# A two-block transformer kernel on one core: memory's keys and values moved into the first attention's stream of products, slabs in another order, the first slab split in quarters, and five waits moved to other engines

## The reference, cut to what matters

```python
h = rms_norm(x, g_norm[l]);  z = h @ w_in[l]
q, k, v, fl, gf, u, gs, qm, gm, gl = split_cols(z)
y_fox = forgetting_attention(q, k, v, log_f) * silu(gf)          # 12 heads of 64
y_s5  = gelu(s5_ssm(u, ...))                                      # complex diagonal state, 48 groups
y_s5  = y_s5 * sigmoid(y_s5 @ w_glu[l] + b_glu[l]) * silu(gs)
kv = rms_norm(mem, g_mem_norm[l]) @ w_mem_kv[l];  mk, mv = split(kv)   # mem is 256 x 1024
y_mem = memory_attention(qm, mk, mv) * silu(gm)                   # 4 heads of 128
gates = sigmoid(gl + b_merge[l])
merged = gates[0]*(y_fox @ w_proj_fox) + gates[1]*(y_s5 @ w_proj_s5) + gates[2]*(y_mem @ w_proj_mem)
x = x + merged @ w_out[l]
```

## Time and profile before

| | us |
|---|---|
| median of three runs | 2324.04 |
| lowest, highest | 2322.27, 2328.61 |
| the profiled execution | 2326.38 |
| its span | 2324.6 |
| busy: PE, DVE, ACT, POOL | 2254.0, 1250.6, 626.4, 1702.5 |

### The profile page before, as it was taken

How to read it: one execution, slowest core, us unless ns; L and a number is a source line. 1 busy time by engine, 2 the same in 40 slices (tenths; PEclk the granted TensorE clock), 3 DMA queues, 4 the chain that set the end, 5 groups by cost and what they waited for, 6 DMA issues and landing times.

```text
span 2324.6 us, 31091 instructions
## 1 busy us (share of the span) xinstructions
PE 2254.0 (97%) x11693; PEld 1827.6 (79%) x11693; DVE 1250.6 (54%) x1804; ACT 626.4 (27%) x1272; POOL 1702.5 (73%) x2692
## 2 busy tenths in 40 slices
PE   7998988999999999999999999999999999999999
PEld 5887766777888888777868888878877777888887
DVE  5976345554443675545668576647645365723121
ACT  3233344332222211444223333201135321300000
POOL 6898161198789899534789888989963378899884
PEclk9999999999999999999999999999999999999999
DMA  6455851423555332211345655523321133432321
GB/s 201 120 135 129 266 173 37 136 82 121 158 166 176 124 112 91 69 46 28 124 144 164 197 173 190 182 90 127 106 90 33 28 113 101 143 111 95 105 91 55
DMA packets 268656, 280.87 MB, mean 121 GB/s; under 512 B 29964, under 2 KB 240592, under 8 KB 268508
## 3 DMA queue, kind: packets, MB, share of 16 engines
q1 hardware_dynamic: 245148, 243.76, 33.8%
q10 hardware_dynamic: 23360, 35.13, 4.7%
HBM read 257.87 MB, written 17.85 MB: 119 GB/s over the span
## 4 chain that ended last, share of the span: by engine, by line
PE 88%; POOL 3%; DVE 3%; DMA 2%; ACT 2%; issue 1%; ACTq 1%; SPq 1%; DVEq 0%; POOLq 0%
PE ps L478 48%; PE ps L641 15%; PE ps L2469 4%; PE ps L2470 4%; PE ps L2471 4%; PE ps L949 2%; PE ps L992 2%; POOL ring_low L249 2%; PE ps L968 2%; PE ps L1121 1%; PE ps L1138 1%; PE ps L1145 1%; POOL ring_high L245 1%; DMA ring<-in_w_in_dram 1%; PE ps L2579 1%
## 5 line engine op out<-in xcount | busy, mean ns | idle before, releaser
L249 POOL TENSOR_TENSOR ring_low<-ring,ring_high 128x256 fp32r<-128x256 f32 x1320 | 1039.7, 818 | 28.5
L245 POOL TENSOR_SCALAR ring_high<-ring 128x256 fp32r<-128x256 f32 x1320 | 623.8, 498 | 517.0 <-PE ps L641 192.2
L478 PE MATMUL ps<-hT_high,ring_high 128*128 128x512 f32 x704 | 279.5, 397 | 5.6 <-POOL ring_low L249 4.1
L478 PE MATMUL ps<-hT_low,ring_high 128*128 128x512 f32 x704 | 275.9, 392 | 0.0
L478 PE MATMUL ps<-hT_high,ring_low 128*128 128x512 f32 x704 | 275.0, 391 | 0.0
L641 PE MATMUL ps<-hT_high,ring_high 128*128 128x512 f32 x568 | 236.2, 416 | 14.7 <-POOL ring_low L249 11.2
L641 PE MATMUL ps<-hT_high,ring_low 128*128 128x512 f32 x568 | 227.3, 400 | 0.0
L641 PE MATMUL ps<-hT_low,ring_high 128*128 128x512 f32 x568 | 226.9, 400 | 0.0
L390 DVE TENSOR_REDUCE ada_acc<-ring 128x256 f32<-128x2048 f32 x48 | 188.1, 3918 | 45.9 <-ACT ring L377 45.8
L478 PE MATMUL ps<-hidden_high,ring_high 128*128 128x512 f32 x512 | 201.0, 393 | 0.0
L478 PE MATMUL ps<-hidden_low,ring_high 128*128 128x512 f32 x512 | 199.6, 390 | 0.0
(11 more groups left out here) (399 smaller groups left out, 4000.9 us busy)
## 6 DMA issues: line engine op xcount, KB each, us to landing
ring<-in_w_in_dram SPq DMA_DIRECT2D x75, 1024.0 KB, 5.3
ring<-in_w_ff_dram SPq DMA_DIRECT2D x64, 1024.0 KB, 5.4
ring<-in_w_ada_dram SPq DMA_DIRECT2D x48, 1024.0 KB, 5.4
ring<-in_w_out_dram SPq DMA_DIRECT2D x12, 1024.0 KB, 5.5
scratch_x<-xT ACTq DMA_DIRECT2D x3, 2048.0 KB, 7.9
ring<-in_w_mem_kv_dram SPq DMA_DIRECT2D x4, 1024.0 KB, 6.2
ring<-in_w_branch_a_dram SPq DMA_DIRECT2D x16, 256.0 KB, 4.1
xT<-scratch_x ACTq DMA_DIRECT2D x2, 2048.0 KB, 9.7
```

The lines of the kernel that those rows point to most:

```text
L245: ins = nc.gpsimd.tensor_scalar(x(hi), x(raw), 1.0, 1.0, ALU.mult, ALU.mult)
L249: ins = nc.gpsimd.tensor_tensor(x(lo), x(raw), x(hi).bitcast(F32), ALU.subtract)
L478: return nc.tensor.matmul(out[0:rows, bank, cols[0]:cols[1]], lhsT, rhs, start=start, stop=stop)
```

## The change

1. **First slab.** POOL splits slab 0 in quarters of two k-tiles, both halves of the columns in turn, and TensorE starts the first two tiles on a quarter instead of on both halves. In `load_stage` the copies of x's turned tiles 2 and 3 go from DVE to ACT, and ACT's others are interleaved with the rounding.
2. **Layout DMAs.** For parts 1 to 4, ACT no longer issues the eight DMAs of the table; SP does, at the front of its turn. The table is copied to SBUF earlier. POOL splits one piece of four of the second half of f's slab.
3. **Slabs.** The four ada slabs after glu_z2, the two mk slabs and the first mv slab are moved behind the last merge slab and out slabs 0, 2 and 3. glu_z0 is issued before SP's turn for the last part, and not behind the reload of y.
4. **Memory in the stream.** The eight tiles of keys and values become the last 64 products of the attention's stream, taken by ACT. The gate of y_fox moves into the attention too, one tile in four steps. `paces` is denser.
5. **Split of y_mem.** ACT rounds, DVE subtracts; POOL no longer does.

```diff
@@ split_weights
+    def first_slab():
+        K.slab_here(pool, 0)
+        for q in range(KD // 2):
+            last = q == KD // 2 - 1
+            for c in range(2):
+                raw = K.slot(0)[:, 2 * q:2 * q + 2, c * P:(c + 1) * P]
+                hi, lo = (x[:, 2 * q:2 * q + 2, :] for x in K.half(0, c))
+                nc.gpsimd.tensor_scalar(hi, raw, 1.0, 1.0, ALU.mult, ALU.mult).then_inc(...)
+                nc.gpsimd.tensor_tensor(lo, raw, hi.bitcast(F32), ALU.subtract).then_inc(...)
...
+        if i == K.first["f"] and c == 1:
+            pieces = pieces[:1]
@@ plan_slabs
     for i in range(3):
         add(f"glu_z{i}", T["w_glu"][0], (0, 768), 0, 768, False, part=i)
-        if i != 1:
+        if i == 0:
             ada(0)
...
         add("mk", T["w_mem_kv"][0], dm, 0, 512, False, part=i)
-        ada(0)
     for i in range(2):
         add("mv", T["w_mem_kv"][0], dm, 512, 512, False, part=i)
-        if i < 1:
-            ada(0)
...
-            if (mp, b) != (3, 2):
-                ada(0)
+            ada(0)
     for i in range(4):
         add("out", T["w_out"][0], dm, 0, D, part=i)
-        if i == 1:
-            ada(0)
+        ada(0)
@@ tiles_stage (VectorE)
+                    early = ada.get(n, []) if n == 0 and arriving is not None else []
+                    for s in early:
+                        ada_add(K, e, s)
@@ s5_stages
     def next_turn(sp, n):
         sp.wait_ge(y_made.sem, n + 1)
-        if n == PARTS - 2:
-            lay_last(sp)
+        if n + 1 < PARTS:
+            lay_next(sp, n + 1)
...
-        K.sync_turns.setdefault(min(slab_at(out_at[n]) + 3, K.first["glu_z0"]), []).append(lambda sp, n=n: next_turn(sp, n))
-    K.sync_turns.setdefault(K.first["glu_z0"], []).append(lambda sp: load_y(sp, PARTS - 1))
+        K.sync_turns.setdefault(min(slab_at(out_at[n]) + 3, K.first["glu_z0"] + (n == PARTS - 1)), []).append(
+            lambda sp, n=n: next_turn(sp, n))
+    K.sync_turns.setdefault(K.first["glu_z0"] + 1, []).append(lambda sp: load_y(sp, PARTS - 1))
...
-                if n < PARTS - 1:
+                if n == 0:
                     lay_toeplitz(n)
                 else:
-                    stream.take(e, out_at[n] - 48)
+                    stream.take(e, pad_at[n] if n < PARTS - 1 else out_at[n] - 48)
@@ fox_stages
+        if n == 10:
+            e.wait_ge(scored.sem, scored0 + 8)
+        if n < 14:
+            return nc.scalar.activation(K.mk[:, n - 10, :], x[:, 0:MEM], ACT.Copy)
+        i, t = divmod(n - 14, 2)
+        return nc.scalar.activation(K.mv[:, t, i * SLAB_W:(i + 1) * SLAB_W], x[:, 0:SLAB_W], ACT.Copy)
...
+    tiles += column_tiles(K, K.first["mk"], 4, KD, K.memT, n=MEM)
...
-            pe.wait_ge(taken.sem, taken.total - len(late))
...
-            for s in late:
-                ada_sum(K, pe, s, 4)
...
+    def gate_of(e, i):
+        m, at = divmod(i - 6, 4)
+        if m >= 0 and at == 0:
+            e.wait_ge(tanh.sem, m + 1)
+            e.wait_ge(out_copied.sem, out0 + 4 * m + 4)
+            gate(K, e, K.y_fox[:, m, :], K.xT[:, m, :], th[:, m % 2, :]).then_inc(gated.sem, 1)
+    paces = [84, 96]
+    for i in range(1, 26):
+        paces.append(min(paces[-1] + (14, 10, 10, 10)[i % 4] if paces[-1] < 235 else paces[-1] + (8, 5, 5, 6)[i % 4], 304))
     attention_stage(K, steps, ..., K.first["gf"], stream,
-                    [84] + [96 + 11 * i // 2 for i in range(24)] + [230, 240, 240])
+                    paces + [304], beside=(tanh_of, gate_of))
@@ mem_stages
-    tiles_stage(K, tiles, 1, dve=dve, also=also, ada_bank=6, late=last, ada_lag=5)
...
-    def split_mem(pool):
-        pool.wait_ge(gated.sem, gated.total)
-        for k in range(12, 16):
-            split_tile(pool, k)
...
+            for k in range(12, 16):
+                e.wait_ge(gated.sem, gated.total - 15 + k)
+                nc.scalar.activation(highs[k], rows_of[k], ACT.Copy).then_inc(mem_rounded.sem, 1)
...
+                v.tensor_tensor(lows[k], rows_of[k], highs[k].bitcast(F32), ALU.subtract).then_inc(mem_split.sem, 1)
@@ load_stage
+    by_scalar = (2, 3, 6, 7, 4, 5)
...
-            evict(2)
-            evict(3)
-            e.wait_ge(by_dve.sem, 4)
+            e.wait_ge(by_dve.sem, 2)
```

More of the change, by code:

```diff
@@ L613, in __init__ @@
         self.seen = set()
-        self.size = len(tiles[0])
+        self.ends = list(itertools.accumulate(len(t) for t in tiles))
         for n, t in enumerate(tiles):
@@ L619, in __init__, with whole @@
         self.taken.total += len(tiles)
+    def whole(self, upto):
+        return sum(1 for end in self.ends if end <= upto)
     def feed(self, pe, upto):
@@ L625, in feed @@
         while self.fed < upto:
-            n, j = divmod(self.fed, self.size)
+            n = self.whole(self.fed)
+            j = self.fed - (self.ends[n - 1] if n else 0)
             if self.arriving is not None and n < 2:
@@ L630, in feed @@
                 if x == 0:
+                    if k % 2 == 0 and k < KD - 2:
+                        pe.wait_ge(K.sig("first_slab_split").sem, k + 2)
+                    if k == KD - 2:
+                        for c in range(2):
+                            K.weight_here(pe, (0, c))
+                            self.seen.add((0, c))
                     pe.wait_ge(self.arriving[0].sem, self.arriving[1] + k + 1)
@@ L636, in feed @@
                     pe.wait_ge(self.taken.sem, self.t0 + before[-1] + 1)
-            if key not in self.seen:
+            if key not in self.seen and (self.arriving is None or n >= 2):
                 self.seen.add(key)
@@ L646, in take @@
     def take(self, e, upto):
-        while (self.took + 1) * self.size <= upto:
+        while self.took < self.whole(upto):
             n = self.took
@@ L861, in norm_stage, with attention_stage @@
     return low, l0, before, 1
-def attention_stage(K, steps, probs, turned, first_slab, stream=None, paces=None):
+def attention_stage(K, steps, probs, turned, first_slab, stream=None, paces=None, beside=None):
     nc, ps = K.nc, K.ps
@@ L1033, in _ @@
                                                  ).then_inc(C.sem, 1)
+                if beside is not None:
+                    beside[0](e, i)
                 if stream is not None and i == U + LAG:
@@ L1075, in _ @@
                     nc.vector.tensor_copy(st["out"], st["whole"](o_view(j))).then_inc(N.sem, 1)
+                if beside is not None:
+                    beside[1](e, i)
     if stream is None:
@@ L2004, in load_stage, with fox_stages @@
     return arriving
-def fox_stages(K, T, late):
+def fox_stages(K, T):
     nc, R, ps = K.nc, K.region, K.ps
@@ L2031, in fox_stages @@
         "halves_made", "mem_squared", "mem_root", "mem_inverted", "mem_scaled", "mem_turned", "mem_copied"))
-    taken = K.sig("ada_taken")
-    before = {name: x for name, x in K.last.items() if name != "ada"}
+    before = dict(K.last)
     with K.stage(before, {}) as block:
@@ L2084, in _ @@
             ins.then_inc(copied.sem, 1)
-            for s in late:
-                ada_take(K, e, s, 4)
     stored.total += 16
@@ L2190, in _ @@
         def _(pe):
+            pe.wait_ge(keys_taken[0], keys_taken[1] - 2)
             stream.feed(pe, 24)
-            for s in last:
-                ada_sum(K, pe, s, 5)
-        @block.vector
-        def _(e):
-            for s in last:
-                ada_take(K, e, s, 5)
     probs = R("mem_probs", [P, 3, 2, MEM], 16384)
@@ L2260, in split_fox_and_s5, with _ @@
             split_tile(pool, k)
-    def split_mem(pool):
-        pool.wait_ge(gated.sem, gated.total)
-        for k in range(12, 16):
-            split_tile(pool, k)
+    mem_rounded, mem_split = K.sig("y_mem_rounded"), K.sig("y_mem_split")
+    with K.stage({}) as block:
+        @block.scalar
+        def _(e):
+            for k in range(12, 16):
+                e.wait_ge(gated.sem, gated.total - 15 + k)
+                nc.scalar.activation(highs[k], rows_of[k], ACT.Copy).then_inc(mem_rounded.sem, 1)
+        @block.vector
+        def _(e):
+            for k in range(12, 16):
+                e.wait_ge(mem_rounded.sem, k - 11)
+                v.tensor_tensor(lows[k], rows_of[k], highs[k].bitcast(F32), ALU.subtract).then_inc(mem_split.sem, 1)
+    mem_rounded.total += 4
+    mem_split.total += 4
+    K.close(vector=mem_split, scalar=mem_rounded)
     K.turn_before(K.position[(K.first["merge00g"], 0)], split_fox_and_s5)
-    K.turn_before(K.position[(K.first["merge01g"], 0)], split_mem)
-    branches = [(highs[a:b], lows[a:b], split.sem, b) for a, b in ((0, 6), (6, 12), (12, 16))]
+    branches = [(highs[a:b], lows[a:b], split.sem, b) for a, b in ((0, 6), (6, 12))]
+    branches.append((highs[12:16], lows[12:16], mem_split.sem, 4))
     return before, branches
```

118 lines of the change are left out of this document (66 added, 52 removed).

## The result

The changed kernel takes 2290.64 us (median of four runs, 2289.61 to 2291.28) where the kernel before, run beside it, took 2323.15. The ratio is 0.9855, with a 95% interval from 0.9838 to 0.9872: 1.45% faster, some 32.5 us of the 41.8 forecast. The profiled execution took 2291.23 us, its span is 2289.4 us, against 2326.38 and 2324.6: 35.2 us less.

The account below looks back on a forecast made before the run. The prediction took the kernel as bound by the amount of TensorE work. Its terms summed to 41.8 us off the profiled 2326.4, giving 2284.6, and 2282 for the median; range 2268 to 2300, its own case 2272 to 2292.

Parts of the forecast that it names:

- Start, 8.5: Kernel start: with slab 0 in quarters the third tile starts at 33.0, not 42.13; 9.1 us, taken as 8.5.
- the rival of the clock: Kernel start: work in short quarters keeps TensorE at 1.2 GHz, so the start's term is 0; 2290.5 us, 7%.
- Layout DMAs, 3.0: Parts before w_glu: TensorE's 3.03 us wait for ACT's late copy goes; net 3.0 us, between -3 and 6.5.
- w_glu, gf0 and the turn, 7.1: Before the attention: earlier glu_z0 gains 4.0 us, gf0's earlier issue 2.0, the dropped ada turn 1.1.
- Attention and memory, 16.0 + 1.0: Keys and values fill the first attention's idle steps, their stage's waits go: 16.0 us; entering memory's attention 1.0.
- Split of y_mem and the merge, 6.5: Merge: POOL, freed of splits, no longer makes TensorE wait; 6.5 us, between 3 and 7.
- Ada slabs among w_out, -0.3: w_out's stage: three more ada slabs fit with some us of margin; -0.3 us, between -6 and 0.
- The slower rival: Ring behind the merge goes serial, 24.4 us a slab pair where TensorE needs 11.0; 54 us lost, 2336 us, 3%.
- The attention keeps its rhythm: First attention: the chain of scores, DVE and ACT sets the step, the 10.1 us idle stay; 2292 us, 12%.
- The start wins nothing: Kernel start: TensorE stays at 1.2 GHz through the quarters and nothing is won; 2290.5 us, 7%.
- SP's turns: Four longer SP turns each hold a slab up and TensorE stands 6.85 us each; 27.4 us lost, 2309.6, 4%.
- POOL slows DVE: Last steps of the first attention: DVE's scalings slow beside POOL, 1.2 us in seven steps, 8 us; 2290, 4%.

Follow-up runs that it names:

- kv_after_attention: The changed kernel with the attention paced as before and the products of keys and values all behind its last step: 2300.75 us, ratio 0.9900.
- gates_in_merge: The changed kernel with w_out's stage as before, four more ada slabs inside merge pairs, and their turned sums taken one tile sooner: ratio 0.9895.
- gates_in_attention: The changed kernel with w_out's stage as in the kernel before and the four left-over ada slabs beside the first attention: 2289.26 us, ratio 0.9848.
- start_alone: The kernel before with only the new start: x's copies dealt anew, first slab split and awaited in quarters: 2319.01 us against 2325.01, ratio 0.9973.
- gates_on_out_before: The kernel before with its three ada slabs of keys and values moved behind w_out's slabs 0, 2 and 3: ratio 1.0006.

## Why the prediction was right, and which steps failed

Direction and range held: 2290.6 lies in 2268 to 2300. The sum was 9 us too good. Term by term it came out as follows; with 6.5 us for the start in place of the 9.3 of the one profile, the leads add up to 32.4 us, which fits the 32.5 of the medians. That the total came within 9 us owes something to luck: the term for w_out was 13 us too good, and a gain of 4.9 us that I had not seen made up for part of it. (The lower ends as I wrote them add up to 7.4 us and not 6.8; the bound of 2317 stays.)

**Start, 8.5: about 6.5.** The mechanism held, quarter by quarter, and the rival of the clock fell: TensorE ran at 2.4 GHz through the quarters. By the Trainium skill, "TensorE: Matmul & The Clock Gate", section "HAM oscillation — how this bites in real kernels", I had made the term 0 in that rival. That was my reading and not the page's case: the example there has waits that are longer than the work between them, and here TensorE stood still for no more than 0.07 us between the quarters, so this trace doesn't test that rule. The size was off because the 39.7 in the sum was that one execution's, with its slab late and its clock at 0.50 from 21.5 us on.

**Layout DMAs, 3.0: 3.0 as lead, 4.1 between two profiles, 1.9 by the ratios.** Right in kind: the wait for ACT's copy went and came back with the old layout, and the wait for v's slab stayed, at 3.5 us. The lead at w_glu's first product holds the end of the 2.27 us wait ahead of it, too, which I had counted in the next term, so the two terms are better read together: 8.9 us where I had put 10.1.

**w_glu, gf0 and the turn, 7.1: 5.9.** The lead went from 12.4 to 18.3.

**Attention and memory, 16.0 + 1.0: 19.2.** Right in kind. 10.5 us are the filling of idle steps, shown by kv_after_attention. The other part was mis-sized: three ada slabs, their turns and the waits behind them cost 8.2 us in the old stage, where I had counted "6.4 us" for the whole stage, the waits for its own slabs and the slow restart included.

**Split of y_mem and the merge, 6.5: 7.0 + 0.9, for another cause.** The size fits, the reason doesn't. Moving the split off POOL gave 1.2 us at most; the rest seems to come from POOL starting its splits at the end of the attention, as its timeline shows.

**Ada slabs among w_out, -0.3 (bounds -6 and 0): -13.4.** This step failed, and it is beyond its own bound. I wrote "DVE's sums of 3.75 us fit" and "I find some us of margin each time". DVE was indeed never the limit for its time. Two things were missing. A slot that holds an ada slab is free after landing, scaling and summing, 12.7 us in gates_in_merge, so three more of them took the ring's advance: w_out's first slab was issued 11.6 us ahead of its use and not 26.0. And the late arrival was paid twice, once as wait and again at 1.2 GHz. w_out's products took 6.4 us more: 2.3 of longer wait, some 3 of low clock, and the rest the turns of three more slabs and a wait for one of them. Another 6.3 us went between the last product and the last of the norm's sums, 1.7 of them as waits. There the clock falls in other kernels too: gates_in_attention, whose w_out stage is the old one, loses 2.5 us in this place. So of the 13.4 us some 10 to 12 are the slabs', and 1.4 to 3.0 are lost without them, for a cause that stays open. The slower rival had this mechanism, with a margin of "about 2 us short"; it was short at the first slab and at the stage's end, and not at each.

**Not in the sum: +4.9.** I wrote that the change touches nothing behind the first block's w_out. It does: the `early` lines of `tiles_stage` let DVE sum the stage's first ada slab before its first tile in every stage with `arriving`, and w_out_2 of the first layer is one. Measured from that stage's first product, DVE's first sum starts 11.9 us behind it before (1154.56 - 1142.65) and 9.2 behind it after (1120.00 - 1110.82), w_out_2's next slab is issued as much sooner, the wait for POOL is 2.2 us and not 4.7, and the clock stays up:

```profile
1135.00:1146.00 11.00, 10.88 (x49) 8.95 (x50) 8.96 (x10) 2.57 (x5) 10.83 (x19) 1.00 0.48 155
```

In start_alone and gates_on_out_before, which lack these lines, the stretch is 52.8 and 53.3 us long (53.8 before); in the changed kernel and in kv_after_attention, which have them, 48.8 and 48.7. No kernel had those lines alone, so this is read from the traces, not tried by itself.

**The rivals.** "The attention keeps its rhythm" fell: 1.5 us of idle are left where 10.1 were, and kv_after_attention brings them back. "The start wins nothing" fell. "SP's turns" fell: TensorE's waits for POOL are 5.0 us and not 27. "POOL slows DVE" left no mark that I could find in the length of an attention of 119.7 us: its 48 scalings of probabilities took 22.0 us and not 20.0. Nothing here isolated it. I had also misread its row: at 500.11 us, where the pair took 0.87 us, POOL was not idle but rounding a slab in pieces of 0.4 us. At 484.39 it was subtracting: the second scaling ran from 484.98 to 486.43, and POOL's subtraction from 485.00 to 486.28. So the two times of that row stand for two instructions of POOL's beside the scalings, and not for POOL and no POOL.

**The rest.** 1.6 us are lost behind w_out_2's stage, spread over several stages; their cause is open.

## What to carry to other kernels

Work that passes through a shared ring has a price in slot time, not in engine time: count for each slab how long it holds its slot, and compare the moment at which the next needed slab is issued with the moment of its use. Moving such work out of one stage moves the bill; ask for the place with the longest idle stretch of the ring, and expect it not to be free there either. And look for every caller of a helper that a change edits, not only the one that it was edited for.

## What was not expected of the hardware

TensorE lost its clock behind a single wait of 3.19 us (granted 0.50 over 695 to 700 us) and behind waits of 1.24 and 0.50 us ahead of the norm's sums (0.50 over 745 to 760), but kept 1.00 behind a wait of 2.2 us at 1135, and behind a 1.43 us wait at 17.95. In gates_in_attention it fell in those sums with no wait ahead of them. The length of the wait alone does not tell. The landing of the first slab differs by 1.9 us between two executions of the same start (13.87 and 15.74), and what follows magnified it to 3.1 us at the third tile.
